# Attention output projections in the joined 512-column form for seven of their eight tiles

## The reference

```python
    o = jnp.einsum("bhsm,bmhd->bshd", p, v.astype(f32)).reshape(bsz, seq, D_MODEL)
    return o.astype(h.dtype) @ w_o
...
        x = x + _memory_cross_attn(_rmsnorm(x, xa_norm[i]), _rmsnorm(mem, xa_mem_norm[i]),
                                   xa_w_q[i], xa_w_kv[i], xa_w_o[i])
        x = x + FFN_RESIDUAL_WEIGHT * _swiglu(_rmsnorm(x, ffn_norm[i, 1]),
                                              ffn_w_gate_up[i, 1], ffn_w_down[i, 1])
```

## Time and profile before

| | us |
|---|---|
| median of three runs | 1281.03 |
| lowest and highest | 1281.02, 1281.09 |
| the profiled execution | 1280.96 |
| its span, first to last instruction | 1279.2 |

### The profile page before, as it was taken

One profiled execution on the slowest core, in us unless ns is written; L12 is line 12 of the kernel. 1 busy time (PEld: TensorE's weight loads), 2 busy tenths in 40 slices (PEclk: granted clock), 3 DMA queues, 4 the chain that ended last, 5 costly groups with the idle time before them and its releaser, 6 DMA issues.

```text
span 1279.2 us, 23313 instructions
## 1 busy us (share of the span) xinstructions
PE 1269.7 (99%) x7946; PEld 1147.6 (90%) x7946; DVE 992.1 (78%) x1565; ACT 763.8 (60%) x1394; POOL 234.9 (18%) x310
## 2 busy tenths in 40 slices
PE   9999999999999999999999999999999999999997
PEld 7888888898899888888888888999999989888887
DVE  6877778897868778768777668999987877787754
ACT  6655654555656556545656447878865656556643
POOL 2433110123001111111111112024421201111111
PEclk9999999999999999999999999999999999999999
DMA  8556645655445556644556647644446554555661
GB/s 277 177 196 196 223 158 170 198 188 168 165 132 181 188 189 204 223 166 156 189 193 212 213 152 261 224 159 136 132 131 203 180 166 142 169 183 194 220 212 46
DMA packets 63094, 232.51 MB, mean 182 GB/s; under 512 B 7024, under 2 KB 8112, under 8 KB 62896
## 3 DMA queue, kind: packets, MB, share of 16 engines
q1 hardware_dynamic: 62368, 230.73, 54.8%
q10 hardware_dynamic: 656, 0.86, 0.2%
HBM read 230.49 MB, written 1.08 MB: 181 GB/s over the span
## 4 chain that ended last, share of the span: by engine, by line
PE 99%; DMA 0%; DVE 0%; issue 0%; ACT 0%; ACTq 0%; DVEq 0%
PE bank L1449 97%; DMA raw<-w_gu 0%; PE bank L1830 0%; PE bank L1802 0%; PE bank L1639 0%; PE bank L1577 0%; DVE w_lo L837 0%; PE bank L1857 0%; DVE final L1344 0%; PE bank L1788 0%; ACT w_hi L410 0%; DVE h L840 0%; ACTq L778 0%; DVE x L837 0%; ACTq L777 0%
## 5 line engine op out<-in xcount | busy, mean ns | idle before, releaser
L837 DVE TENSOR_TENSOR w_lo<-raw,w_hi 128x1024 fp32r<-128x1024 f32 (+2 forms) x403 | 522.5, 1299 | 28.3 <-ACT w_hi L410 27.9
L410 ACT ACTIVATE w_hi<-raw 128x1024 fp32r<-128x1024 f32 (+2 forms) x403 | 442.0, 1098 | 90.8 <-PE bank L1449 83.3
L1449 PE MATMUL bank<-h,w_hi 128*128 128x512 f32 (+1 forms) x1808 | 432.4, 383 | 1.2 <-DVE h L840 1.1
L1449 PE MATMUL bank<-a,w_hi 128*128 128x256 f32 (+1 forms) x1878 | 381.6, 324 | 0.3 <-DVE w_lo L837 0.2
L1449 PEld LDWEIGHTS bank<-h,w_hi 128*128 128x128 f32 x1808 | 326.1, 189 | 59.5 <-DVE h L840 1.7
L1449 PEld LDWEIGHTS bank<-a,w_hi 128*128 128x128 f32 x1878 | 312.5, 190 | 26.3 <-issue 0.5
L1449 PE MATMUL bank<-a,w_lo 128*128 128x256 f32 x1280 | 256.4, 283 | 0.0
L1449 PE MATMUL bank<-h,w_lo 128*128 128x256 f32 x1736 | 242.6, 282 | 0.0
L1449 PEld LDWEIGHTS bank<-h,w_lo 128*128 128x128 f32 x1736 | 231.9, 191 | 10.6
L410 ACT ACTIVATE corr<-bank 128x256 f32<-128x256 f32 x255 | 96.1, 377 | 207.5 <-PE bank L1449 207.3
L1449 PEld LDWEIGHTS bank<-a,w_lo 128*128 128x128 f32 x1280 | 201.0, 191 | 2.7
(11 more groups left out here) (201 smaller groups left out, 1014.6 us busy)
## 6 DMA issues: line engine op xcount, KB each, us to landing
raw<-w_gu SPq DMA_DIRECT2D x174, 512.0 KB, 3.5
raw<-w_down SPq DMA_DIRECT2D x64, 704.0 KB, 4.4
raw<-w_xbc SPq DMA_DIRECT2D x32, 512.0 KB, 3.6
raw<-w_conv_in SPq DMA_DIRECT2D x24, 512.0 KB, 3.9
raw<-w_q SPq DMA_DIRECT2D x16, 512.0 KB, 4.1
raw<-w_k SPq DMA_DIRECT2D x16, 512.0 KB, 3.5
raw<-w_v SPq DMA_DIRECT2D x16, 512.0 KB, 3.5
raw<-w_o SPq DMA_DIRECT2D x16, 512.0 KB, 3.8
```

What stands on the lines that cost most here:

```text
L410: return nc.scalar.activation(out, in_, ACT.Copy, scale=scale)
L837: return nc.vector.tensor_tensor(out, a, b, op)
L1449: return nc.tensor.matmul(out, lhs, rhs, start=start, stop=stop, skip_group_check=check)
```

## The change

Tiles 0 to 6 of both output projections are computed with `pairs`, in the same three pieces for tiles 0 to 2, so that a piece now does its 512-column matmuls first and its 256-column ones behind them. Tile 7 stays in the separate form. `ready` makes tile 0 wait for the heads' outputs before each block. On DVE, tiles 0 to 6 get one more addition: first the bank's second half is added to x, finished (`step`), and then the first half, which raises `evac` as before. ACT does nothing more: there is no `corr` copy.

```diff
@@ project_out, VectorE
                     else:
                         dve.wait_ge(unit_done, n0 + k + 1)
+                        if k < KT - 1:
+                            step(tt(x[:, k, :], bank[b][:, SEQ:], x[:, k, :], ALU.add))
                         tt(x[:, k, :], bank[b][:, 0:SEQ], x[:, k, :], ALU.add).then_inc(evac[b], 1)
@@ output_tile, TensorE
-                for k in range(k0, k1):
-                    if t == 0 and k % 2 == 0:
-                        pe.wait_ge(o_ready, HEADS * layer + k // 2 + 1)
-                    w = slice(k * P, k * P + P)
-                    ins = three(bank[t % 4][:, 0:SEQ], w_hi[n % SLOTS][:, w], w_lo[n % SLOTS][:, w], a[:, 0, k, :], a[:, 1, k, :],
-                                k == 0, k == KT - 1)
+                ready = (lambda k: (o_ready, HEADS * layer + k // 2 + 1)) if t == 0 else None
+                if t < KT - 1:
+                    ins = pairs(bank[t % 4], n % SLOTS, a, range(k0, k1), 0, k0 == 0, k1 == KT, ready)
+                else:
+                    for k in range(KT):
+                        w = slice(k * P, k * P + P)
+                        ins = three(bank[t % 4][:, 0:SEQ], w_hi[n % SLOTS][:, w], w_lo[n % SLOTS][:, w], a[:, 0, k, :], a[:, 1, k, :],
+                                    k == 0, k == KT - 1)
```

## The result

The changed kernel takes 1286.23 us, the median of six executions (1285.00 to 1288.54), against 1281.11 of the kernel before beside it: 1.004 of the time, with a 95% interval of 1.003 to 1.005. It is slower, as forecast, but by 5.1 us and not by 3.6, and above the top of the range (1285.4). The profiled execution took 1285.97 us with a span of 1284.2. Two executions, of 1784.82 and 2556.64 us, in the first series of the experiment that fills the wait, are far off all others and are left out of its median and ratio.

A forecast was written before the change was run, and what follows sets the result against it. TensorE was taken as the bound, busy 1269.7 of 1279.2 us. VectorE's lateness, with TensorE's gain counted in, loses 1.81 us in each of two layers, together 3.6: 1280.96 + 3.6 = 1284.6 us, range 1283.2 to 1285.4.

The forecast's parts named there:

- the range: Whole kernel: 1283.2 to 1285.4 us, from the bounds of the added operation (1283.3 and 1285.1) with 0.3 for release times.
- TensorE's gain, 0.585 us a layer: Output projection: joined tiles take 2.79 us against 2.88, seven times 0.09 less 0.045 for a wait on low probabilities.
- VectorE's second addition, 0.46, and 2.82 us a tile: Output projection, VectorE: the added operation raises a tile from 2.35 to 2.81 to 2.82 us, so VectorE no longer catches up.
- Rivals 1 and 2: VectorE's tiles: second addition costs only 0.33, 1283.3 us, chance 0.07; or VectorE catches up, 1279.8 us, chance 0.05.
- The chain to block 6, at 393.45, and 1.81 us lost a layer: Opening of gu1: late h_lo of tile 6 delays block 6 from 391.64 to 393.45, TensorE waiting 2.3 us.
- What the splits cost TensorE on the way: Before gu1: its first unit's split ends at 389.67, costing TensorE at most a tenth, inside the larger wait.
- So nothing further is late: Behind block 6 of gu1's opening: h_lo of tile 7, sum of squares and later splits all arrive before they are wanted.
- Rival 3: Opening after the wait: TensorE's clock falls to 1.2 GHz, costing 3.5 us more a layer, 1291.6 us; chance 0.04.
- The forecast case: Both layers: VectorE's pace causes the loss, 3.6 us together, time 1284.6 us; chance 0.82, with rival 4 in it.

The follow-up runs named there:

- the experiment that fills the wait: Changed kernel plus eight 512-column matmuls into an unused bank before block 6 of gu1's and gu3's openings: 1284.64 us first series, 1284.56 us second.
- TensorE's half alone: Against the kernel before: joined form on TensorE, VectorE keeping its one addition a tile (second bank half left out of x): 1280.37 us, ratio 0.999.
- the kernel with VectorE's addition alone: Kernel before, TensorE in separate form, plus one finished addition a tile on VectorE into an unused buffer, tiles 0 to 6: 1285.37 us, ratio 1.0029.
- changed kernel again: The changed kernel, unaltered, measured a second time on one chip beside the kernel with the wait filled: 1285.72 us, ratio 1.0039.
- the third addition: Changed kernel plus a third finished addition per tile on VectorE, into an unused buffer: 1293.15 us, ratio 1.0086.

## Why the prediction was right, and where it was wrong

- **TensorE's gain, 0.585 us a layer.** Right: 0.51 against 0.54 in the stretch measured, with TensorE's half alone. By the fixed 2.5 ns a matmul of the Trainium skill, page "TensorE: Matmul & The Clock Gate", section "Wait — 56ns, not 53.3ns?", an estimate gives 0.02 us a tile. The trace does not agree: with TensorE's half alone the joined tiles 3 and 4 start 2.79 us apart (376.38 and 379.17), 0.09 less than 2.88, and the rows decide.
- **VectorE's second addition, 0.46, and 2.82 us a tile.** Right: 2.81, and 0.79 for a pair, which is 0.46 + 0.33. Rivals 1 and 2 did not happen; h_lo stayed at 0.96.
- **The chain to block 6, at 393.45, and 1.81 us lost a layer.** Right: 393.48, and 1.84 in the layer where the clock holds. What the splits cost TensorE on the way was set too low. The prediction priced only that of `gu1`'s first unit, at a tenth at most; but tiles 3 to 6 took 11.38 us in all (375.76 to 387.14), 2.90 for tile 3, where four times 2.79 are 11.16. The opening began at 390.02 where 389.68 (389.77 with this execution's offset of 0.09) was forecast. It made the visible wait shorter, 1.9 us instead of 2.3, and the loss no larger, as the text said.
- **"So nothing further is late".** Right as to waits: the trace has none behind block 6. VectorE's two splits after h_lo of tile 7 ended at 397.6 and not at 397.1, beside another GpSimd addition, and nothing waited for them.
- **Rival 3, the clock, at 0.04 and at 1291.6.** This is the step that failed: the sum put the effect of the wait on TensorE's clock at nothing. The forecast case held for 3 of 11 executions, at 1284.8 to 1285.0. In the others, by their time and clock, the clock fell once or twice. I had set the rival's chance low because of an idle stretch of 1.06 us at a granted clock of 1.00. That row said nothing on an idle stretch twice as long, and in another execution the very wait of that row lasted 2.12 us and the clock did fall behind it. The price was wrong too, in the other direction: 1.56 us a fall, not 3.5, and not in each layer. Seen from the result, with the measured price and an even chance in each of two layers, 1.6 us belong on top of 1284.6, which gives 1286.2; the rows of before could not have given that chance.
- **The range.** It held the bounds of the sum but left the clock out as one of the 2 in 10. With one fall inside, its top would have been 1287. (Its lower end, by its own sum of 1283.3 and 0.3 for the release times, should have been 1283.0; nothing hangs on it.)

The Trainium skill, page "TensorE: Matmul & The Clock Gate", section "HAM oscillation — how this bites in real kernels", holds that waits of TensorE let its clock fall and that what comes after starts slow. The windows above agree in kind, 0.50 after an idle stretch of 1.9 us; the waits of that section's example are longer, about 3 to 5 us. In this case it happened at some waits of 1.9 to 2.1 us and not at others.

What stays open: what decides, at one length of the wait, whether the clock falls. The changed kernel's 1.90 us did both within one execution, and 2.10 us at the start of one kernel had no fall where 2.12 us in another had one. Open too is why the kernel with VectorE's addition alone, waiting 1.68 us, shows no fall in nine executions and the changed kernel at least one in eight of eleven; their runs were on different chips.

## What to carry to other kernels

Before giving an engine work in order to spare the busiest one, write down its pace against the producer's and the reserve that it has built up by the end of the phase; here 0.5 us a tile were just what let VectorE catch up, and the price came one phase later, at the first thing that needed its last result. Moving that first thing only hands the lateness to the next item in the late engine's order, so the whole order behind it must be checked, with the length that each operation has beside its new neighbours. And a new idle stretch of some 2 us on TensorE should be priced twice: its length, and a chance of a fall of the clock behind it. The kernel before, executed more often, has times of 1282.2 to 1283.9 us at a mean clock of 0.997; more than three executions and a second trace of it might have shown that chance ahead of the forecast.

## What the runs showed of the hardware that I had not expected

- An idle stretch of 1.9 us on TensorE was followed by a granted clock of 0.50 in some executions and by 1.00 in others, even within one execution (layer 0 fell and layer 1 did not, and the reverse in the second profile). Each of these falls cost 1.5 to 1.6 us. Keeping TensorE busy with unused matmuls in that time ended the falls in the opening at no cost: 33.03 against 33.01 us over the opening, and 1284.56 against 1285.72 us.
- The fall does not come at a fixed moment. In the five traced falls the clock went down 0.3 us (changed kernel, layer 0) to 1.5 us (changed kernel again, layer 1) after TensorE had resumed, and once, in layer 1 with the third addition, 0.4 us before, still within the wait.
- VectorE's split of 1024 columns took 1.76 us instead of 1.22 when GpSimd's addition had started 0.06 us before it, and h_lo 0.48 instead of 0.96 when it had none beside it. The Trainium skill, page "SBUF — State Buffer", section "Who interferes with whom", has the two engines share a port pair that is locked while one uses it; the rows agree in kind, 0.54 us lost in the 0.68 us (392.62 to 393.30) that the two ran side by side.
